# The mLSTM heads' feature sums from split tiles instead of fp32 tiles

## What is computed

```python
def layernorm32(x, eps):
    x32 = x.astype(jnp.float32)
    xc = x32 - jnp.mean(x32, axis=-1, keepdims=True)
    return xc * lax.rsqrt(jnp.mean(xc * xc, axis=-1, keepdims=True) + eps)
...
    h = mlstm_chunkwise(heads(q), heads(k) * (M_HEAD_DIM ** -0.5), heads(v_pre), log_i, log_f)
    h = layernorm32(h, LN_EPS).transpose(0, 2, 1, 3).reshape(bsz, seqlen, M_WIDTH)
    return (jax.nn.sigmoid(o_pre.astype(jnp.float32)) * h * head_g).astype(q_pre.dtype)
```

## Time and profile before

| | |
|---|---|
| median of 3 runs | 1914.2 us (1913.11 to 1914.75) |
| profiled execution | 1912.57 us, its span 1910.8 us, so 1.8 us lie around the span |
| mean granted TensorE clock | 0.997 of full speed |
| PE busy | 1888.8 us, 99% of the span |
| DVE busy, ACT busy | 1020.6 us (53%), 795.0 us (42%) |
| stage of the change | about 600 to 800 us from the span's start |

### The profile page before, as it was taken

The page is one execution under the profiler, slowest core; times in us unless marked ns, Lnnn a source line. Parts: engine busy times, 40 slices in busy tenths (PEclk is TensorE's granted clock), DMA queues, the critical chain, the costliest instruction groups (busy, mean ns, idle before and its releaser), DMA issues.

```text
span 1910.8 us, 21285 instructions
## 1 busy us (share of the span) xinstructions
PE 1888.8 (99%) x8721; PEld 1561.5 (82%) x8721; DVE 1020.6 (53%) x1279; ACT 795.0 (42%) x1061; POOL 228.2 (12%) x258
## 2 busy tenths in 40 slices
PE   9999999999999999999999999999999999999997
PEld 7888888888888788888888888888878888888885
DVE  5444444357355666664444344655565777774335
ACT  5323222246444656442322323556564444443234
POOL 2000001201300111130000023101004100000212
PEclk9999999999999999999999999999999999999999
DMA  4422322342241222423232222322213323223231
GB/s 167 158 99 90 109 91 97 114 144 99 74 147 66 77 92 85 144 95 104 89 100 99 100 99 89 121 67 67 74 38 110 100 88 109 90 95 105 98 111 55
DMA packets 51937, 188.98 MB, mean 99 GB/s; under 512 B 6568, under 2 KB 6824, under 8 KB 50944
## 3 DMA queue, kind: packets, MB, share of 16 engines
q1 hardware_dynamic: 46656, 166.22, 25.8%
q0 software_dynamic: 4176, 19.82, 3.0%
q10 hardware_dynamic: 1008, 1.58, 0.2%
HBM read 179.18 MB, written 11.03 MB: 100 GB/s over the span
## 4 chain that ended last, share of the span: by engine, by line
PE 94%; DVE 3%; ACT 2%; issue 1%; DMA 0%; DVEq 0%; ACTq 0%
PE psum L1733 93%; ACT at L800 1%; DVE wl L1139 1%; DVE zv L1136 0%; ACT wh L800 0%; PE psum L2116 0%; DVE x L1133 0%; DMA wraw<-in_w_ffn 0%; DVE vl L1139 0%; DVE at L1494 0%; DVE mg L1133 0%; DVE sl L1139 0%; ACT L796 0%; DVE us L1133 0%; ACT us L800 0%
## 5 line engine op out<-in xcount | busy, mean ns | idle before, releaser
L1733 PE MATMUL psum<-xh,wh 128*128 128x512 f32 x1760 | 694.0, 394 | 1.6 <-DVE xl L1136 0.8
L1733 PE MATMUL psum<-xh,wl 128*128 128x512 f32 x1760 | 685.3, 389 | 0.0
L1733 PE MATMUL psum<-xl,wh 128*128 128x512 f32 x1760 | 685.1, 389 | 0.0
L1139 DVE TENSOR_TENSOR wl<-wraw,wh 128x1024 fp32r<-128x1024 f32 (+1 forms) x314 | 401.1, 1285 | 398.1 <-ACT wh L800 397.0
L800 ACT ACTIVATE wh<-wraw 128x1024 fp32r<-128x1024 f32 (+1 forms) x314 | 325.6, 1047 | 361.6 <-PE psum L1733 359.7
L1733 PEld LDWEIGHTS psum<-xh,wh 128*128 128x128 f32 x1760 | 330.4, 188 | 77.6 <-issue 9.3
L1733 PEld LDWEIGHTS psum<-xl,wh 128*128 128x128 f32 x1760 | 330.5, 188 | 69.9 <-issue 2.9
L1733 PEld LDWEIGHTS psum<-xh,wl 128*128 128x128 f32 x1760 | 330.4, 188 | 69.5
L1592 POOL TENSOR_TENSOR ssq<-x 128x512 f32<-128x512 f32 x5 | 5.2, 1040 | 714.1 <-DVE x L1218 454.0
L1733 PE MATMUL psum<-wh,xh 128*128 128x512 f32 (+1 forms) x256 | 88.3, 345 | 0.4 <-ACT zv L800 0.4
L1733 PE MATMUL psum<-wh,xl 128*128 128x512 f32 (+1 forms) x256 | 86.0, 336 | 0.0
(11 more groups left out here) (307 smaller groups left out, 2216.0 us busy)
## 6 DMA issues: line engine op xcount, KB each, us to landing
wraw<-in_w_ffn SPq DMA_DIRECT2D x86, 512.0 KB, 3.2
wraw<-in_w_down SPq DMA_DIRECT2D x44, 512.0 KB, 3.2
wraw<-in_w_up SPq DMA_DIRECT2D x44, 512.0 KB, 3.4
wraw<-in_w_qg SPq DMA_DIRECT2D x28, 512.0 KB, 3.3
wraw<-in_w_att SPq DMA_DIRECT2D x24, 512.0 KB, 3.2
wraw<-in_w_dn SPq DMA_DIRECT2D x22, 512.0 KB, 3.3
wraw<-in_w_zu SPq DMA_DIRECT2D x16, 512.0 KB, 3.2
wraw<-in_w_zv SPq DMA_DIRECT2D x8, 512.0 KB, 3.6
```

The lines of the kernel that those rows point to most:

```text
L1139: return e.tensor_tensor(dst, src, hi.bitcast(F32), ALU.subtract)
L1733: return e.matmul(dst, lhsT, rhs, start=start, stop=stop, skip_group_check=skip)
```

## The change

The two products with ones are made from split fp32r tiles. In `T` 0 and `T` 4, right behind VectorE's addition, ScalarE now copies `tm(4)` to `sh[:, 0:512]` and VectorE subtracts to get `sl[:, 0:512]`. `T` 1 and `T` 5 are two fp32r products with `onesr` instead of one fp32 product with `ones`. `MIX_AT` moves `T` 1 and `T` 5 (and some neighbours) later.

```diff
-    (103, 1): "H0.7", (103, 2): "T0.0 H1.m", (103, 3): "T0.1", (104, 0): "T0.2", (105, 3): "T0.3 T0.4",
+    (103, 1): "H0.7", (103, 2): "T0.0 H1.m", (104, 0): "T0.1", (104, 1): "T0.2", (105, 3): "T0.3 T0.4",
...
-    (109, 1): "H1.6", (110, 2): "H1.7", (110, 3): "G0 G1 T1.0", (111, 0): "T1.1",
-    (111, 1): "T1.2 T1.3", (111, 2): "T1.4 H2.m", (111, 3): "T1.5", (112, 0): "T1.6",
+    (109, 1): "H1.6", (110, 2): "H1.7", (110, 3): "G0 G1 T1.0", (111, 1): "T1.1",
+    (111, 2): "T1.2 T1.3 H2.m", (111, 3): "T1.4", (112, 1): "T1.5 T1.6",
...
-    (119, 2): "T2.4 H3.m", (119, 3): "T2.5", (120, 0): "T2.6", (122, 0): "H3.0 T2.7",
+    (119, 2): "T2.4 H3.m", (120, 0): "T2.5 T2.6", (122, 0): "H3.0 T2.7",
...
-    (126, 0): "T3.0", (126, 3): "T3.1", (127, 0): "T3.2", (127, 1): "T3.3", (127, 2): "T3.4", (127, 3): "T3.5",
-    (128, 0): "T3.6", (129, 0): "T3.7", (129, 3): "G6 G7",
+    (126, 0): "T3.0", (126, 3): "T3.1", (127, 0): "T3.2", (127, 1): "T3.3", (127, 2): "T3.4",
+    (128, 0): "T3.5 T3.6", (129, 0): "T3.7", (129, 3): "G6 G7",
...
@@ ScalarE @@
-                if s == 3:
+                if s == 0:
+                    e.wait_ge(*t_d.at(h, "add"))
+                    act(sh[:, 0:512], tm(4), ACT.Copy).then_inc(t_a.sem, 1)
+                elif s == 3:
...
                     act(tm(4), hn[:, 2 * h + 1, :], ACT.Square).then_inc(t_a.sem, 1)
+                    e.wait_ge(*t_d.at(h, "sq"))
+                    act(sh[:, 0:512], tm(4), ACT.Copy).then_inc(t_a.sem, 1)
@@ VectorE @@
                     e.tensor_tensor(t4, h0, h1, ALU.add).then_inc(t_d.sem, 1)
+                    e.wait_ge(*t_a.at(h, "sh"))
+                    low(sl[:, 0:512], t4, sh[:, 0:512]).then_inc(t_d.sem, 1)
...
                     e.tensor_tensor(t4, t4, tm(5), ALU.add).then_inc(t_d.sem, 1)
+                    e.wait_ge(*t_a.at(h, "ch"))
+                    low(sl[:, 0:512], t4, sh[:, 0:512]).then_inc(t_d.sem, 1)
@@ TensorE @@
-                if s == 1:
-                    e.wait_ge(*t_d.at(h, "add"))
-                    mm(bank(7), ones[:, :], tm(4)).then_inc(t_p.sem, 1)
-                elif s == 5:
-                    e.wait_ge(*t_d.at(h, "sq"))
-                    mm(bank(7), ones[:, :], tm(4)).then_inc(t_p.sem, 1)
+                if s in (1, 5):
+                    e.wait_ge(*t_d.at(h, "cl" if s == 5 else "sl"))
+                    mm(bank(7), onesr[:, :], sh[:, 0:512], True, False)
+                    mm(bank(7), onesr[:, :], sl[:, 0:512], False, True).then_inc(t_p.sem, 1)
```

More of the change, by code:

```diff
@@ L680, in _build @@
     t_p = sig("s_t_p", T=lambda h, s: {1: [(h, "sum")], 5: [(h, "cs")]}.get(s, []))
-    t_a = sig("s_t_a", T=lambda h, s: {3: [(h, "sq0")], 4: [(h, "sq1")], 6: [(h, "ln"), (h, "R")]}.get(s, []))
-    t_d = sig("s_t_d", T=lambda h, s: {0: [(h, "add")], 2: [(h, "c0"), (h, "c1")], 4: [(h, "sq")],
+    t_a = sig("s_t_a", T=lambda h, s: {0: [(h, "sh")], 3: [(h, "sq0")], 4: [(h, "sq1"), (h, "ch")], 6: [(h, "ln"), (h, "R")]}.get(s, []))
+    t_d = sig("s_t_d", T=lambda h, s: {0: [(h, "add"), (h, "sl")], 2: [(h, "c0"), (h, "c1")],
+                                       4: [(h, "sq"), (h, "cl")],
                                        6: [(h, "u")], 7: [(h, "n0"), (h, "n1")]}.get(s, []))
```

## The result

The changed kernel takes 1921.99 us (median of 4 runs, 1921.46 to 1923.58), the kernel before 1913.94 (4 runs, 1913.11 to 1914.75). The ratio is 1.0044, with a 95% interval of 1.0033 to 1.0056: slower by more than the 0.2% that can be told here. The profiled execution took 1921.75 us (span 1920.0, mean granted clock 0.995), 9.18 us more than the one of before, where 9.2 were forecast; the medians lie 8.05 apart. The forecast time was 1923.4, so the median is 1.4 us under it, at the very edge of the 1922 to 1925 that the forecast gave as its own range.

The account below looks back on a forecast made before the run. PE was taken to bound the kernel (busy 1888.8 of 1910.8 us). Terms -3.4 + 1.5 + 7.7 + 2.3 - 0.1 + 0.5 + 0.7 = +9.2 on 1914.2 gave 1923.4 us; own range 1922 to 1925 (82%), wider 1920.5 to 1926.5.

Parts of the forecast that it names:

- The products: PE's eight products with ones: each 0.42 us cheaper as two fp32r products, 3.4 us less in all.
- `T0.4`: Head 0: ACT's copy delays the exponentials, so PE's last six score products wait; added wait 1.5 us.
- `T1.4`: Head 1: square, addition and both parts come behind `qkev`; PE waits from 666.0 to 673.7, 7.7 us added.
- The clock: Behind head 1's long wait: lower clock until 5.0 us after PE resumes, costing 2.3 us (bounds 1.6 to 2.4).
- estimate of 0.8 us: Alternative clock price from the skill's 1.67 us of throttled time per gap, half lost; not the one adopted.
- Later places: Three places where PE takes operands just in time: head 2's scores -0.1, head 3's +0.5, unit 132 +0.7 us.
- head 3's scores: Head 3's score products: PE arrives earlier and ACT's table load is 0.1 later; +0.5 us, wait about 0.6.
- unit 132: PE takes `wl` at unit 132: its chain starts 0.1 us earlier, PE comes 0.84 earlier; +0.7 us.
- The first parts of the heads: `T` 1 products in the heads: no new waits; the forecast fails if they wait too.
- Head 2's scores: Head 2's score products: a 0.1 us wait for the last `qkev` subtraction goes, -0.1 us.
- The sum: Whole kernel: -3.4 + 1.5 + 7.7 + 2.3 - 0.1 + 0.5 + 0.7 = +9.2 us.
- total of 1922.0: Whole kernel: the time if the clock term were 0.8 us, by the skill's throttled time per gap.

Follow-up runs that it names:

- the first experiment: The change with `T1.4` alone put back to (111, 2), ahead of `qkev`, against the kernel before: 1914.24 us, ratio 1.0006.

## Why the prediction was right, point by point

**The products:** a pair takes 0.45 us, as forecast. The gain per product was a little larger than forecast: from `H1.m`'s product to the next `rowr,sel`, with one product of ones between and no wait, it was 619.13 - 604.00 = 15.13 us and is 619.31 - 604.63 = 14.68. That is 0.45 instead of 0.42, or 3.6 us for all eight.

**`T0.4`:** 1.43 us of wait in the list, 1.7 from start to start, against 1.5. ACT's copy ran at 627.90, behind DVE's addition, and the split and the exponentials moved by that. With the copy on VectorE, and the squares where they were, the wait is gone.

**`T1.4`:** 7.54 us of wait in the list. PE's product could have started at 666.73 + 0.227 = 666.96 and started at 674.66, 7.70 us later, and 7.7 was the forecast. PE's place was right too: the shift of everything ahead is 0.95 us, which puts the forecast's 666.0 and 673.7 at 667.0 and 674.7. The experiments show that it is the cause: with `T1.4` ahead, or `T1.5` later, the 8 us are gone; with the new order alone 7.5 of them are there.

**The clock:** this term was mis-sized. I had 2.3 us, from a lower clock lasting until 5.0 us after the resumption; it lasted 3.9, and the price is 1.8 (1.76 by products, 1.81 by the stage), inside the bounds of 1.6 to 2.4. The error was to count the 5 us of the earlier trace rows from the resumption. In the earlier trace rows the clock fell only 1.7 us after PE had resumed, so its low stretch was 3.3 us. For the earlier trace rows the trace gives a granted clock of 1.00, so those rows show slow products and no low clock. Here the fall came inside the wait, and part of the low stretch passed while PE had nothing to do. What lay behind the resumption was not the same each time: 3.9 us in the change, 3.6 behind the same wait of 7.54 us with `T0.4` behind the exponentials, 3.2 with the new order alone. What ends the low stretch isn't shown. The prediction's estimate of 0.8 us, from the 1.67 us of throttled time that the Trainium skill gives for a gap (TensorE: Matmul & The Clock Gate, HAM oscillation — how this bites in real kernels), is less than half of what this gap cost; its direction is borne out. (Its total of 1922.0 adds up to 1921.9.)

**Later places:** 0.62 us of wait at head 3's scores and 0.66 at unit 132, against 0.6 and 0.7. The first parts of the heads (`T` 1) didn't wait, as forecast. Head 2's scores were mis-sized: forecast was a gain of 0.1 us, measured is 0.5. Besides the short delay ahead of them, of 0.13 us, the 24 products themselves took 690.85 - 686.72 = 4.13 us before and take 700.56 - 696.76 = 3.80 now. They take 3.80 to 3.82 in all five kernels in which PE starts them without a delay.

**The sum** can be made for the stage from start to start, stretch by stretch, before against after. It is -3.6 (products) + 1.7 (`T0.4`) + 7.9 (`T1.4`) + 1.8 (clock) - 0.5 (head 2's scores) + 0.6 (head 3's) + 0.8 (unit 132) = 8.7, and 8.72 are measured. A late operand costs more than the length in the list. At unit 132, where the list has 0.66, the waiting product starts 1.05 us after the one ahead (805.59 to 806.64) and the next one 0.34 behind it, where the pace is 0.227 for each: 0.93 lost. The forecast had these terms as -3.4, 1.5, 7.7, 2.3, -0.1, 0.5 and 0.7. So its errors, of up to 0.5 us, partly cancel. That 9.18 between the profiles meets the forecast's 9.2 so closely is partly chance: outside of the stage +0.6, -1.1 and +0.9 came on top, which have nothing to do with the change.

## What to carry to other kernels

On engines that work strictly in order, cost a new step not by its duration but by what stands ahead of it and behind it on its engine, and by whether its consumer moved as far as it did: 0.45 us saved eight times was lost here to one step that slipped behind an evacuation while its consumer didn't follow. Work added on half-idle engines isn't free in a kernel without slack; the cheaper form of it was the one that stays on one engine. And when a wait is removed, look up the next operand that PE will now reach too early, before counting the gain.

## What the runs showed of the hardware that I had not expected

Waits of the same length, amid the same work, bring the clock down in one profiled execution and not in another. All nine kernels have the wait of 1.7 us for ACT's `az` between 1418 and 1431 us, with the same work around it. From its product (`ones,az`) to the one with `tml` at the end, this is before, the change, and the first experiment, in PE's timelines:

```profile
1420.57 1.05 PE L1733 MATMUL psum<-ones,az 128*128 128x1 f32 x8 [1.72 <-ACT az L800]
...
1899.15 1.12 PE L1733 MATMUL psum<-tml,ones 128*128 128x512 f32 x2 [1.41 <-ACT tml L800]
```

```profile
1429.99 1.05 PE L1743 MATMUL psum<-ones,az 128*128 128x1 f32 x8 [1.70 <-ACT az L801]
...
1907.43 2.07 PE L1743 MATMUL psum<-tml,ones 128*128 128x512 f32 x2 [1.41 <-ACT tml L801]
```

```profile
1422.16 1.46 PE L1743 MATMUL psum<-ones,az 128*128 128x1 f32 x8 [1.69 <-ACT az L801]
...
1902.38 1.12 PE L1743 MATMUL psum<-tml,ones 128*128 128x512 f32 x2 [1.44 <-ACT tml L801]
```

From start to start that is 478.58 us, 477.44 and 480.22. In the change (and with `T0.4` behind the exponentials) the clock stayed up, and the 1.7 us cost nothing more; in six kernels it fell for 3 to 3.5 us, at a cost of 1.1 to 1.2; with `T1.4` ahead it was low for 6.5 us and cost 2.8:

```profile
1422.50:1429.00 6.50, 6.50 (x24) 5.73 (x24) 2.56 (x6) 1.36 (x4) 0.00 (x0) 0.51 0.00 0
```

In the same way the last product, with `tml`, takes 1.12 us in six kernels and 1.68 to 2.08 in the other three, behind the same 1.4 us wait. In these three the clock fell during the wait or the product, in the six only when PE had finished. From its start to the end of the span it is 1910.8 - 1899.15 = 11.65 us before and 1920.0 - 1907.43 = 12.57 in the change. In the stage of the change no wait up to 1.64 us was followed by a fall, one of 1.73 was, and with those of 6.2 and 7.5 us (three of three) it always came, 2.5 to 4.6 us into the wait. At the kernel's start the run with `T1.5` later had a wait of 1.94 us that was followed by one. What decides in the case of short waits isn't known from these runs.

These nine profiles are of nine programs, one execution each. That it also differs between executions of one program is suggested by the 27 runs of the kernel before: those with a mean granted clock of 0.997 took 1912.29 to 1913.56 us (17 runs), those with 0.996 took 1913.11 to 1915.09 (10). So 2 to 3 us can lie between two executions, which is nearly as much as this change could have gained: a difference of that size between two profiles has to be looked for in the stage that was changed, and not in the total.
